# First stage rewritten, a ring of 17 weight slots, and no matmuls on zeros: a decoder step on eight cores

## What is computed

```
h    = rmsnorm(x, pre_g)
proj = h @ w_in                       # 1024 -> 6400 columns: u v z_a | p z_b | xc bg cg z_c
A: vn = rmsnorm(v);  a = u * (tril(w_s) @ vn + b_s)      per chunk of 128 rows, 6 heads
B: d  = mean over a trailing window (2, 4, 8, 16) of p, minus p;  b = (d @ w_pg) * pool_scale
C: c  = bg * conv3(cg * xc)
mix  = [a * silu(z_a), b * silu(z_b), c * silu(z_c)]     # 2048 columns
x    = x + rmsnorm(mix @ w_out, post_g)
```

## Time and profile before

| what | value |
|---|---|
| median of 3 runs | 2041.59 us (2038.41 to 2043.72) |
| profiled execution | 2042.29 us, its longest span 2041.2 us (core 7) |
| spans of the cores | 2033.0 to 2041.2 us, mean granted clock 0.993 to 0.995 |
| PE busy on core 7 | 2003.8 us, 98% |
| DVE, ACT, POOL busy | 57%, 31%, 26% |
| DMA, core 7 | 309.61 MB as written, mean 152 GB/s; HBM read 409.48 MB |

### The profile page before, as it was taken

How to read it: one execution, slowest core, us unless ns; L and a number is a source line. 1 busy time by engine, 2 the same in 40 slices (tenths; PEclk the granted TensorE clock), 3 DMA queues, 4 the chain that set the end, 5 groups by cost and what they waited for, 6 DMA issues and landing times.

```text
span 2041.2 us, 38277 instructions; the slowest of 8 cores (2033.0 to 2041.2 us)
## 1 busy us (share of the span) xinstructions
PE 2003.8 (98%) x12288; PEld 1186.2 (58%) x12288; DVE 1170.5 (57%) x1937; ACT 629.5 (31%) x1560; POOL 522.4 (26%) x1032
## 2 busy tenths in 40 slices
PE   6999999999999999999999999999999999999997
PEld 3655565566566466557656546656755655664673
DVE  3754665576565475466575546547657544653763
ACT  3332333323323232232332332323333222232231
POOL 3521421231331131132142123113214212211310
PEclk8999999999999999999999999999999999999999
DMA  9998697788797876859879868686988985758862
GB/s 205 195 191 158 164 211 115 167 150 157 184 182 126 171 162 94 118 147 198 132 198 167 130 167 155 94 158 125 196 166 171 154 123 158 114 82 149 143 114 75
DMA packets 200498, 309.61 MB, mean 152 GB/s; under 512 B 84848, under 2 KB 90096, under 8 KB 198768
## 3 DMA queue, kind: packets, MB, share of 16 engines
q0 software_dynamic: 90912, 174.66, 55.9%
q1 hardware_dynamic: 109104, 131.46, 23.7%
q10 hardware_dynamic: 288, 1.05, 0.2%
HBM read 409.48 MB, written 55.99 MB: 228 GB/s over the span
## 4 chain that ended last, share of the span: by engine, by line
PE 93%; DMA 2%; DVE 2%; issue 2%; ACT 0%; POOL 0%; DVEq 0%; ACTq 0%; POOLq 0%
PE ps L566 61%; PE ps L676 23%; PE ps L536 7%; DMA sb_ring<-w_in 2%; PE ps L763 1%; PE ps L654 1%; DVE sb_pw L386 1%; DMA sb_cstb<-cstb 1%; DVE sb_mix L390 0%; ACT sb_scr L382 0%; DVE sb_scr L390 0%; POOL sb_stats L401 0%; DVE sb_hin L390 0%; DVE sb_xs L386 0%; PE ps L518 0%
## 5 line engine op out<-in xcount | busy, mean ns | idle before, releaser
L566 PE MATMUL ps<-sb_hT,sb_ring 128*128 128x384 bf16 (+1 forms) x8448 | 1329.0, 318 | 9.0 <-DMA sb_ring<-w_in 4.7
L566 PEld LDWEIGHTS ps<-sb_hT,sb_ring 128*128 128x128 bf16 x8448 | 824.7, 98 | 475.8 <-issue 17.9
L382 ACT ACTIVATE sb_scr<-ps 128x384 f32<-128x384 f32 (+3 forms) x664 | 371.1, 563 | 1077.2 <-PE ps L566 508.4
L347 POOL DMA_DIRECT2D sb_ring<-w_in x552 | 296.0, 542 | 919.0 <-PE ps L566 746.8
L676 PE MATMUL ps<-sb_wout,sb_mix 128*128 128x512 bf16 x2176 | 471.6, 379 | 0.0
L676 PEld LDWEIGHTS ps<-sb_wout,sb_mix 128*128 128x128 bf16 x2176 | 212.9, 98 | 255.4
L390 DVE SCALAR_TENSOR_TENSOR sb_scr<-sb_pw,sb_convw,sb_scr 128x384 f32<-128x384 f32 (+1 forms) x336 | 182.1, 542 | 145.3 <-ACT sb_ccarry L382 109.0
L386 DVE TENSOR_TENSOR sb_scr<-ps,sb_scr 128x384 f32<-128x384 f32 (+1 forms) x288 | 151.8, 530 | 131.7 <-PE ps L763 94.9
L399 POOL TENSOR_SCALAR sb_stats<-sb_stats 128x1 f32<-128x1 f32 x204 | 59.0, 289 | 560.0 <-ACT sb_scr L382 555.4
L390 DVE SCALAR_TENSOR_TENSOR sb_hout<-sb_xs,sb_stats,sb_pre_bc 128x1024 bf16<-128x1024 f32 x62 | 79.6, 1284 | 177.7 <-POOL sb_stats L401 177.7
L536 PE MATMUL ps<-sb_ring,sb_hT 128*128 128x512 bf16 (+1 forms) x1088 | 178.8, 326 | 0.0
(11 more groups left out here) (48 smaller groups left out, 501.0 us busy)
## 6 DMA issues: line engine op xcount, KB each, us to landing
sb_ring<-w_in POOLq DMA_DIRECT2D x528, 256.0 KB, 8.5
xd<-sb_xs SPq DMA_DIRECT2D x51, 512.0 KB, 3.5
sb_xs<-xd SPq DMA_DIRECT2D x51, 512.0 KB, 8.6
sb_wout<-w_out POOLq DMA_DIRECT2D x64, 256.0 KB, 12.7
sb_xs<-x_p SPq DMA_DIRECT2D x31, 512.0 KB, 12.0
hd<-sb_hout SPq DMA_DIRECT2D x62, 256.0 KB, 3.9
sb_ring<-w_in POOLq DMA_DIRECT2D x12, 1024.0 KB, 8.4
y_p<-sb_xs SPq DMA_DIRECT2D x16, 512.0 KB, 3.5
```

Of the source, the lines that this page charges most:

```text
L347: emit(POOL, lambda g: g.dma_start(out=flat, in_=src), writes=a.res, dsem=ds, extra=[prev_tok] if prev_tok else [])
L382: return emit(ACT, lambda a: a.activation(out=out, in_=in_, func=func, scale=scale, **kw), reads=reads, writes=writes)
L566: ins = pe.matmul(bank(b, N), lhsT=wa.ap[:, k, :], rhs=hT[:, k, j0 * 128:j0 * 128 + N], start=(k == 0), stop=(k == 7))
```

## The change

Seven edits, all but the second and the last in the first pass alone:

- `warm_up` keeps the one ACT instruction that loads its table and loses the memset and the matmuls on zeros.
- The ring has 17 slots instead of 14. The room comes from `hin`, which becomes a view of `mix` (blocks 12 to 15, which are written in the C phase).
- x0, the gains `pre_bc` and x1 to x3 are issued on SP in this order; before, the gains and x2 were issued on ACT.
- The ring's first load waits for x2, the second for x3, the third and fourth for x4 (before: x0, x1, x2, x2). `pump` comes behind the transposition of tile 3.
- The p jobs of the first three tiles alternate with the normalisation and transposition of tiles 3 to 5; the hooks of that phase are written out.
- In the first pass no `w_out` piece is issued behind v jobs or behind h = 0 and 1, one behind each of h = 2 to 5, and three behind each c until all sixteen are out (c = 3).
- The sample tile's `vn` is written first, straight from the matmul's bank, and the copy that goes out after it, in all four layers; the cast is gone.

```diff
-NSLOT = 14
+NSLOT = 17
...
-        hin = sb("hin", [128, NHI, D], BF16)
...
+        hin = mix[:, 12:16, :].rearrange("p k t -> p (k t)").rearrange("p (s d) -> p s d", s=NHI)
...
             act(stats[:, 0:1], czero[:, 0:1], AF.Square, reads=[R["czero"]], writes=[R_stat[0]])
-            emit(DVE, lambda v_: v_.memset(mix[:, 0, 0:512], 0.0), writes=R_mix[0])
-
-            def fill(pe):
-                for _ in range(24):
-                    ins = pe.matmul(bank(7), lhsT=mix[:, 0, 0:128], rhs=mix[:, 0, 0:512], start=True, stop=True)
-                return ins
-            emit(PE, fill, reads=R_mix[0], writes=[bank_res[7]])
...
+            dve_stt(vn[:, j, :], vps, rs, vg_bc[:], ALU.mult, ALU.mult,
+                    reads=[bank_res[b], bank_res[b + 1], R_stat[si], R["vg_bc"]], writes=[R_vn[j]])
+            if is_s:
                 dve_stt(stg, vps, rs, vg_bc[:], ALU.mult, ALU.mult,
                         reads=[bank_res[b], bank_res[b + 1], R_stat[si], R["vg_bc"]], writes=R_sv)
                 emit(SP, lambda q: q.dma_start(out=vs_o[l], in_=stg), reads=R_sv, dsem=d_vs)
-                dve_copy(vn[:, j, :], stg, reads=R_sv, writes=[R_vn[j]])
...
-                load_pre(0, ACT)
-                sl = [load_x(0, 0), load_x(0, 1)]
-                sl += [load_x(0, 2, ACT), load_x(0, 3)]
+                sl = [load_x(0, 0)]
+                load_pre(0)
+                sl += [load_x(0, 1), load_x(0, 2), load_x(0, 3)]
...
                 warm_up()
-                after_x(0)
-                ring_try_alloc()
-                norm_rows(sl[0], hin[:, 0, :], R_hin[0])
-                after_x(1)
-                ring_try_alloc()
-                norm_rows(sl[1], hin[:, 1, :], R_hin[1])
+                nr(0)
+                nr(1)
                 sl.append(load_x(0, 4))
-                t_job(0, 0)
+                tj(0)
                 after_x(2)
                 ring_try_alloc()
+                nr(2)
+                sl.append(load_x(0, 5))
+                tj(1)
+                after_x(3)
                 ring_try_alloc()
...
+                nr(3)
+                tj(2)
                 setup_loads()
                 load_vg(0)
...
+                pj(0, 0)
+                after_x(4)
+                ring_try_alloc()
+                ring_try_alloc()
+                nr(4)
+                pj(1, 0)
+                tj(3)
+                pump()
+                nr(5)
+                pj(2, 0)
+                tj(4)
+                pj(3, 0)
+                tj(5)
+                for gi in range(4):
+                    pj(gi, 1)
+                    release(wsched[(g, l)][("p", gi)])
+                    pool_vec(g, l, gi)
+                    later_pop(2 if gi else 0)
...
-                if wo:
+                if wo and pi > 0:
                     wout_piece(l, wo.pop(0))
...
-                if wo:
+                if wo and (pi > 0 or h >= 2):
                     wout_piece(l, wo.pop(0))
...
-                if wo:
-                    wout_piece(l, wo.pop(0))
+                for _ in range(3 if pi == 0 else 1):
+                    if wo:
+                        wout_piece(l, wo.pop(0))
```

More of the change, by code:

```diff
@@ L553, in v_job @@
                 emit(SP, lambda q: q.dma_start(out=vs_o[l], in_=stg), reads=R_sv, dsem=d_vs)
-                dve_copy(vn[:, j, :], stg, reads=R_sv, writes=[R_vn[j]])
-            else:
-                dve_stt(vn[:, j, :], vps, rs, vg_bc[:], ALU.mult, ALU.mult,
-                        reads=[bank_res[b], bank_res[b + 1], R_stat[si], R["vg_bc"]], writes=[R_vn[j]])
         def in_job(b, wa, sts_i):
@@ L876, in run_pass @@
             if pi == 0:
-                load_pre(0, ACT)
-                sl = [load_x(0, 0), load_x(0, 1)]
-                sl += [load_x(0, 2, ACT), load_x(0, 3)]
+                sl = [load_x(0, 0)]
+                load_pre(0)
+                sl += [load_x(0, 1), load_x(0, 2), load_x(0, 3)]
                 def after_x(k):
-                    POOL.h.wait_ge(d_xs[k].sem, 16)
-                    POOL.waited[id(d_xs[k].sem)] = 16
-                warm_up()
-                after_x(0)
-                ring_try_alloc()
@@ L887, in run_pass, with nr, tj @@
-                norm_rows(sl[0], hin[:, 0, :], R_hin[0])
-                after_x(1)
-                ring_try_alloc()
-                norm_rows(sl[1], hin[:, 1, :], R_hin[1])
+                    n = 16 * (1 + k // NX)
+                    POOL.h.wait_ge(d_xs[k % NX].sem, n)
+                    POOL.waited[id(d_xs[k % NX].sem)] = n
+                def nr(k):
+                    norm_rows(sl[k], hin[:, k % NHI, :], R_hin[k % NHI])
+                def tj(k):
+                    t_job(k, k % NHI)
@@ L891, in run_pass, with pj @@
+                def pj(gi, si_):
+                    p_job(g, l, gi, si_)
+                warm_up()
+                nr(0)
+                nr(1)
                 sl.append(load_x(0, 4))
-                t_job(0, 0)
+                tj(0)
                 after_x(2)
                 ring_try_alloc()
+                nr(2)
+                sl.append(load_x(0, 5))
+                tj(1)
+                after_x(3)
                 ring_try_alloc()
-                norm_rows(sl[2], hin[:, 2, :], R_hin[2])
@@ L897, in run_pass @@
-                sl.append(load_x(0, 5))
-                t_job(1, 1)
-                after_x(3)
-                pump()
+                nr(3)
+                tj(2)
                 setup_loads()
                 load_vg(0)
-                t_job(2, 2)
-                def hook(i):
-                    if i < 3:
-                        norm_rows(sl[3 + i], hin[:, i, :], R_hin[i])
-                    if i >= 1 and i < 4:
-                        t_job(2 + i, i - 1)
-                    later_pop(2 if i > 4 else 0)
@@ L911, in run_pass @@
-                pool_phase(g, l, [(gi, si_) for si_ in range(2) for gi in range(4)], hook)
+                pj(0, 0)
[16 more added lines that the diff above has]
+                    later_pop(2 if gi else 0)
```

## The result

The changed kernel took 2079.26 us (median of its series), the kernel before 2043.72 in the same series; the ratio is 1.0131, 95% interval 1.0087 to 1.0176. The forecast was 2042.7 with a range of 2031 to 2050: it missed, on the slow side.

What follows compares the result with a forecast made beforehand. First pass taken as bound by a never-empty DMA queue beside TensorE. Core 0's output jobs start at 177.2 (174.8 + 2.4) against 173.57, +3.6; with -1.5 for `vn`, span 2042.3; plus 0.4, 2042.7 us, range 2031 to 2050.

Steps and rivals of the forecast that it cites:

- Clock behind the wait: Output jobs after the `w_out` wait: lower clock costs 2.4 us, bounds 1.2 to 4.8.
- What is late next: End of first pass: last `w_out` piece lands at 174.4 (core 7) and 174.8 (core 0); TensorE waits some 13 us.
- No matmuls on zeros: Kernel start: removing 24 matmuls and a memset changes the time by 0; bounds nothing or 2.4 us.
- Order of the first loads and jobs: Kernel start: v jobs start near 37.5 instead of 44.37, 6.9 us won on TensorE's clock.
- 26.7 us for ten: Kernel start: landing time of the ten p and v slots, carried over from the kernel before, less 3 us.
- as late as 44: Rival at the start: v's weights land at 44 us, output jobs reached at 168, same time; no chance of its own.
- w_out moved: First pass: the 4.7 us ring wait and 2.3 us of lower clock go; first v job to output jobs takes 124.3.
- The count of ten pieces: First pass: ten `w_out` pieces leave the queue ahead of the load that was waited for, 16 us.
- The sample tile's vn: Spatial jobs in the three passes that waited: writing `vn` first gives -1.5 us, bounds -2.0 and 0.
- Ring of 17 in later passes: Later passes: no waits for the ring there, so nothing to win, 0.
- no change: Whole kernel: core 0 slowest, 2042.7 us, the start's gain given back at the output jobs; chance 0.60.
- two waits instead of one: Rival at c = 0 to 3: ring runs dry, clock falls twice, 2048.7 us; chance of over 2047.7: 0.16.

Runs made afterwards that it cites:

- r1: The changed kernel run again without edits, in a later series; 1.0036 of the kernel before.
- r3: The changed kernel run a fourth time without edits; 1.0040 of the kernel before (the third time, between them, gave 1.0042).
- e3: The kernel before without its 24 matmuls on zeros and their memset, nothing else; 0.9986 of the kernel before.
- e2: The changed kernel with the 24 matmuls on zeros and their memset put back, nothing else; 1.0047 of the kernel before.
- e13: The changed kernel, with SP waiting for v's weights to land before it issues the loads behind them; 1.0040 of the kernel before.
- e1: The changed kernel with the `w_out` pieces issued where the kernel before has them, ring still 17 slots; 1.0036 of the kernel before.
- e6: The changed kernel with the `w_out` pieces where the kernel before has them and a ring of 14 slots; 1.0000 of the kernel before.
- e5: The changed kernel with five `w_out` pieces instead of three behind each first-pass spatial job, all ahead of v's 1024 KB; 1.0015 of the kernel before.
- e8: The changed kernel with hT's six transposing loads for the next pass issued behind the first output job; 1.0038 of the kernel before.
- e7: The kernel before with `vn` written directly where the spatial jobs read it, and without the zeros; 1.0000 of the kernel before.
- e4: The kernel before with only the last `w_out` piece held back until the last spatial job of the first pass; 1.0081 of the kernel before.

## Why the prediction was wrong, step by step

The median missed by 36.6 us, and two steps failed. *Clock behind the wait* knew two levels of the clock, and a third, with nothing set down for it, took some 30 us. *What is late next* had the last piece of `w_out` on core 0 4.6 us too early (174.8, measured 179.4). The second alone ends at the upper edge of the range: without the stretch the changed kernel took 2048.78 us once in the first series, and 7.4 to 8.6 us more than the kernel before in r1 to r3, where the sum had nothing. The second's mechanism is shown, though not what made it so long; the cause of the first stays open.

*No matmuls on zeros: 0.* Right (e3, and e2 against r1 to r3).

*Order of the first loads and jobs: v jobs at 37.5.* Wrong; they began at 47.7 on core 0 (44.3 on the earliest core). The first ring issue was sized well, 13.16 against 12.5. The step that failed is "26.7 us for ten" with 3 us of credit: it carried over the landing time of the kernel before, but the ring's second to fourth load now wait for x3 and x4, v's two stand behind a later row's normalisation on POOL, at 24.76, and SP by then has put in other loads ahead of them or beside them (2.7 MB between 18 and 27 us). With these held back v does land at 36 to 40 (e13). The rival that v lands "as late as 44" came true, and its clause was right as well: the time does not hang on it.

*w_out moved: no ring wait, no cold clock in 120 to 132, TensorE 7.0 us less on its way.* Right: 47.67 to 172.4 are 124.7 us, against 124.3 forecast. The count of ten pieces was too high, though: on core 7 nine had been issued ahead of the load of 90.88, and ahead of c = 1 thirteen stood before and seven now.

*What is late next.* Right in kind, and e1 against e6 shows the mechanism: 17 slots let v's 1024 KB ahead of the last pieces, 14 do not. Wrong in size. The term was 5.6 us, bounds 4.9 to 6.4; it measured 8.2 (e5 against r1). The last piece landed at 179.4 on core 0 where 174.8 was forecast, and on core 7 at 172.3 where 174.4 was; the median of the eight cores went from 166.5 to 177.0. The bounds were bytes over the rate of the whole queue, but the piece that comes last is not the mean of the queue: on core 5 the piece next to last landed at 172.3, the last one at 179.3, both issued within 0.6 us. What holds it back is not shown: it is not hT's packets (e8), and not the loads ahead alone, as e5 has as many ahead as e6 and lands 2.4 us behind it (172.5 and 170.1). The wait itself was shorter than forecast, 7.2 us and not 13, as TensorE came 10 us later; its end is what counts.

*Clock behind the wait: 2.4 us, bounds 1.2 to 4.8.* Right: 43.90 against 41.4, 2.5 us.

*The sample tile's vn: -1.5.* The waits fell as forecast, by 2.0 us; in the time no gain could be shown (e7).

*Ring of 17 in later passes: 0.* Right: on core 0 no matmul behind the start waits for the ring.

Repaired, the sum for core 0 reads 179.67 - 173.57 + 2.5 - 0.9 = 7.7 us (the 0.9 is what is left over), and r1 to r3 measured 7.4 to 8.6. Here "no change" was already wrong: 0.4% can be told from none. The rival "two waits instead of one" had the price nearly right (2048.7), but by luck, as the place was wrong: TensorE was never short of weights in c.

*What no step had: the stretch at 0.81.* It is some 30 of the 36.6 us by which the median missed. Nothing in the trace of before has a third level of the clock, and I priced the wait by its length and by the two levels seen. The experiments say what it does not follow from: not from the wait (e2, e4, r1), nor from the missing zeros with it (r1 to r3), nor from two cores of a pair coming back close together (r1, as far as each core's own time tells). It is not the changed kernel's own either: one execution of the kernel before (2067.54 us, in the series of e1 to e4) had cores 0 and 1 at a mean clock of 0.977, which fits such a stretch, and the others at 0.989 to 0.994. Over all executions, those left out too, some cores were under 0.986 in 6 of 7 of the changed kernel in the first series, in 4 of 19 in r1 to r3, and in 28 of 113 of the kernel before in the five later series. That speaks for the occasion and not for the code. But in the first series six of seven executions of the kernel before were free of it, by their times (2038.41 to 2044.68 us, and 2413.36); whether the idle stretch of the changed kernel helped it to start there stays open (which chip the first series had is not recorded). It could not be tried, since the stretch never came back in a profiled execution.

## What to carry to other kernels

Where a transfer queue is full for the whole of a stage, count the bytes that stand ahead of the last transfer the stage waits for, before and after, and forecast the end of the stage from that first; here it named the right wait, and was 2.6 us short. What is won elsewhere in such a stage was given back there (e13). A deeper prefetch ring is not free in such a stage: it moves the next stage's loads in front of this one's last. And when a median is off by far more than any wait in the profile, look at the granted clock core by core and run the same kernel again before explaining it by the code.

## What the runs showed of the hardware that I had not expected

A granted clock of 0.8125 of full speed for 160.5 us on both cores of one pair, while the other six of the chip ran at 1.00 with the same work (786 against 963 matmuls). It set in some 4 us after the clock had returned from 0.50. The Trainium skill ("TensorE: Matmul & The Clock Gate", "Seeing it yourself") describes a peak-current limiter of 13/16, 0.8125, that takes a whole die once three of its cores run dense matmuls, and holds it while the load lasts. The level agrees. For the rest the executions differ: in one of the changed kernel (2447.53 us) cores 0 to 3 had mean clocks of 0.813 to 0.815 over the whole time, which fits what the Trainium skill says, and one of the kernel before (2447.59 us) had cores 4 to 7 at 0.810 to 0.812. But in most executions all eight cores ran the same matmuls for 2 ms at 0.99, and in the profiled one the level came on one pair alone, and let go after 160.5 us with the load still on.

Pieces of one queue, issued within 0.6 us of each other, landed 7 us apart on core 5 (172.3 and 179.3), at a DMA share of 1.09: here the share tells that the engines are full, not when the last of a set arrives.
